# The out-projection of two attention layers in seven block products instead of eight

## What is computed

```python
h = rms_norm(x, norm_g[i]); proj = h @ w_in[i]
...
r_out = silu(rz) * retention(rotary(rq), rotary(rk), rv)
m_out = silu(mz) * moba(rms_norm(mq), rms_norm(mk), mv, rel_bias)
y = concatenate([r_out, m_out], axis=-1) @ w_out[i]
x = x + y
gate = sigmoid(rms_norm(x) @ w_ple_gate[i])
e = rms_norm(p[i] @ w_ple[i], ple_norm_g[i])
x = x + gate * e
```

## Time and profile before

| | |
|---|---|
| median of 3 runs | 1584.13 us (1581.85 to 1585.59) |
| the profiled execution, its own time | 1584.45 us |
| its span, first to last instruction | 1582.7 us |
| granted TensorE clock, mean | 0.952 of full speed |
| PE busy | 1331.9 us, 84% of the span |
| PEld (weight loads beside PE) | 717.9 us, 45% |
| DVE busy | 422.3 us, 27% |
| ACT busy | 278.8 us, 18% |
| POOL busy | 180.1 us, 11% |
| HBM read | 495.11 MB, 314 GB/s over the span |

### The profile page before, as it was taken

The page is one execution under the profiler, slowest core; times in us unless marked ns, Lnnn a source line. Parts: engine busy times, 40 slices in busy tenths (PEclk is TensorE's granted clock), DMA queues, the critical chain, the costliest instruction groups (busy, mean ns, idle before and its releaser), DMA issues. The chain is left out here.

```text
span 1582.7 us, 22176 instructions
## 1 busy us (share of the span) xinstructions
PE 1331.9 (84%) x9378; PEld 717.9 (45%) x9378; DVE 422.3 (27%) x838; ACT 278.8 (18%) x544; POOL 180.1 (11%) x122
## 2 busy tenths in 40 slices
PE   9999999999999999776776777899999676667676
PEld 4855456545869564322322323655654232232232
DVE  3443343523555531020000000257321000010011
ACT  2132310323413121210000000105211011011010
POOL 0450033300000005692000000000000000000000
PEclk9999999999999999899888899999999989899889
DMA  9923442244631489999999999944799999999997
GB/s 382 342 81 145 178 156 106 80 186 161 238 123 59 165 338 426 427 429 428 428 429 428 428 429 428 392 180 167 284 379 426 426 428 426 428 428 427 427 428 325
DMA packets 44868, 498.20 MB, mean 315 GB/s; under 512 B 6657, under 2 KB 8961, under 8 KB 12545
## 3 DMA queue, kind: packets, MB, share of 16 engines
q1 hardware_dynamic: 44800, 497.22, 76.7%
HBM read 495.11 MB, written 2.10 MB: 314 GB/s over the span
## 5 line engine op out<-in xcount | busy, mean ns | idle before, releaser
L2834 PE MATMUL banks<-weight_ring,arena 128*32 128x512 f32 x1472 | 214.6, 716 | 127.6 <-DMA weight_ring<-in_moe_weights 127.4
L2762 DVE TENSOR_TENSOR arena<-arena,banks 64x512 f32<-64x512 f32 x32 | 22.1, 690 | 665.3 <-ACT arena L2707 665.3
L2834 PEld LDWEIGHTS banks<-weight_ring,arena 128*32 128x32 f32 x1472 | 45.6, 120 | 283.9 <-DMA weight_ring<-in_moe_weights 142.2
L2819 PE MATMUL banks<-arena,x 128*128 128x64 f32 x1024 | 120.4, 277 | 0.0
L2819 PEld LDWEIGHTS banks<-arena,x 128*128 128x128 f32 x1024 | 119.7, 196 | 0.1
L323 PE MATMUL banks<-weight_ring,hT 128*128 128x512 f32 x256 | 114.0, 601 | 0.0
L2707 ACT ACTIVATE arena<-banks 64x512 f32<-64x512 f32 x32 | 18.9, 591 | 501.8 <-PE banks L2834 501.8
L2845 PE MATMUL banks<-weight_ring,arena 128*32 128x512 f32 x728 | 86.0, 596 | 22.2 <-DMA weight_ring<-in_moe_weights 10.2
L2875 PE MATMUL banks<-arena 64*128 64x512 f32 x240 | 59.6, 615 | 21.0 <-ACT arena L2713 21.0
L323 PEld LDWEIGHTS banks<-weight_ring,hT 128*128 128x128 f32 x256 | 48.7, 192 | 58.4 <-issue 58.0
L2834 PE MATMUL banks<-arena 128*32 128x512 f32 x352 | 58.6, 686 | 16.8 <-DMA arena<-in_moe_weights 16.8
(11 more groups left out here) (526 smaller groups left out, 1738.5 us busy)
## 6 DMA issues: line engine op xcount, KB each, us to landing
weight_ring<-in_moe_weights SPq DMA_DIRECT2D x137, 2048.0 KB, 27.0
weight_ring<-in_ring_weights SPq DMA_DIRECT2D x35, 2048.0 KB, 9.3
arena<-in_moe_weights SPq DMA_DIRECT2D x18, 2048.0 KB, 44.5
spare_weights<-in_moe_weights SPq DMA_DIRECT2D x10, 2048.0 KB, 43.9
mix<-in_moe_weights SPq DMA_DIRECT2D x9, 2048.0 KB, 48.2
arena<-in_moe_weights SPq DMA_DIRECT2D x17, 1024.0 KB, 42.2
x_normed<-in_moe_weights SPq DMA_DIRECT2D x9, 1024.0 KB, 39.1
hT<-in_moe_weights SPq DMA_DIRECT2D x9, 1024.0 KB, 47.5
```

Of the source, the lines that this page charges most:

```text
L2762: dve.tensor_tensor(hid[0:2 * CAP, :], sil[0:2 * CAP, :], b_gu[2 * CAP:4 * CAP, :], ALU.mult).then_inc(s_h, 1)
L2819: ins = pe.matmul((b_x, b_dn)[k // 4][:, k % 4 * 2 * CAP:(k % 4 + 1) * 2 * CAP], g.x[:, tt, k * P:(k + 1) * P], Pr[:, tt, :], start=(tt == ...
L2834: ins = pe.matmul(b_gu[q:q + CAP, :], xg[:, 2 * quarter + k, e * CAP:(e + 1) * CAP], up_w(where, quarter, e)[:, which, k, :], start=(quart ...
```

## The change

The out-projection is now itself one set of seven block products, `out_product` O1 to O7 of four matmuls each, with GpSimd forming four sums of the two weight chunks 8 and 9 (the same 128x2048 shape, into the ring and into T2 and T3), and four sums of mixT (SO1 to SO4, 128x512, in `rqk_flat`). O1 and O2 share bank 0, O6 and O7 use bank 1, O5 and O4 bank 4, O3 bank 5. ScalarE copies O1's block out (`y_p1_copy`); VectorE forms u_a and u_b and adds them and the products into x: nine additions of 128x512 in place of four. The two embedding products e_in(0) and e_in(1) move in between O2 and O6, and between O7 and the transposes. Gate products go to banks 0, 5, 4, 1. The right half of tile 1 is finished before its left half, and its squares are taken in that order. Places 8 and 9 of the ring are freed by O4 and O3.

```diff
--- before.py
+++ after.py
@@ -351,9 +351,9 @@
     def sems(g, name):
         return [g.sem(f"{name}_{k}") for k in ("squares", "eps", "root", "xs", "transposed", "hT")]
 
-    def squares(self, act, tt, ch):
+    def squares(self, act, tt, ch, place=None):
         half = slice(ch * HALF, (ch + 1) * HALF)
-        j = 2 * tt + ch
+        j = 2 * tt + (ch if place is None else place)
         act.activation(self.g.xs[:, tt, half], self.g.x[:, tt, half], ACT.Square,
                        accum_out=self.part[:, j:j + 1]).then_inc(self.s_sq.sem, 1)
 
...
@@ -407,12 +407,13 @@
...
-                 ("cd", "combined", 12), ("sl", "combined_used", 6), ("ts", "weight_sums", 8), ("as_", "input_sums", 4), ("rot", "rotated", 4), ("mean", "qk_mean", 2),
+                 ("cd", "combined", 12), ("sl", "combined_used", 6), ("ts", "weight_sums", 12), ("as_", "input_sums", 8),
+                 ("yc", "y_p1_copied", 1), ("u", "y_sums", 5), ("rot", "rotated", 4), ("mean", "qk_mean", 2),
...
-                 ("mix", "mixed", 2), ("mt", "mix_transposed", 4), ("mT", "mixT", 4), ("y", "y", 4), ("x", "x", 4),
+                 ("mix", "mixed", 2), ("mt", "mix_transposed", 4), ("mT", "mixT", 4), ("y", "y", 7), ("x", "x", 4),
...
@@ -497,7 +498,7 @@
     for l in range(DEPTH):
         q = layer[l]
         for i, when in enumerate((q.prj(3), q.prj(4), q.prj(6), q.prj(8), q.prj(15), q.prj(15), q.prj(22), q.prj(22),
-                                  q.y(3), q.y(4), q.e(4), q.g(3), q.g(4))):
+                                  q.y(7), q.y(5), q.e(4), q.g(3), q.g(4))):
             g.free_when[per * l + i] = when
 
 
@@ -517,7 +518,12 @@
                               (q.c11(1), formed(q, 0, C12), formed(q, 0, C21), formed(q, 0, C22)))
     gates_ready = lambda q: ((q.c11(2), q.sl(4), q.sl(6), q.sl(5)) if q is layer[0] else
                              (q.c11(2), q.sl(1), q.sl(3), q.sl(2)))
-    OUT_BANK = (0, 1, 4, 5)
+    GATE_BANK = (0, 5, 4, 1)
+    O1, O2, O6, O5, O3, O7, O4 = range(1, 8)
+    MX11, MX12, MX21, MX22 = (g.mixT[:, 4 * k:4 * k + 4, t * P:(t + 1) * P] for t in range(2) for k in range(2))
+    SO1, SO2, SO3, SO4 = (rqk_flat[:, i * 512:(i + 1) * 512].rearrange("p (k t) -> p k t", k=HT) for i in range(4))
+    u_a, u_b = tmp[:, 0:512], tmp[:, 512:1024]
+    X11, X12, X21, X22 = (g.x[:, tt, ch * HALF:(ch + 1) * HALF] for tt in range(2) for ch in range(2))
     part = lambda j: (slice(None), j // 2, slice((j % 2) * HALF, (j % 2 + 1) * HALF))
 
     with nc.Block() as block:
@@ -621,11 +627,15 @@
                 act.activation(eroot[:, tt:tt + 1], epart[:, 2 * tt + 1:2 * tt + 2], ACT.Sqrt,
                                bias=eeps[:, tt:tt + 1], scale=1.0 / D).then_inc(q.er.sem, 1)
 
+            def y_p1_copy(q):
+                act.wait_ge(*q.y(O1))
+                act.copy(u_a, ps[0]).then_inc(q.yc.sem, 1)
+
             def sigmoid(q, j):
                 act.wait_ge(*q.g(j + 1))
                 if j >= 2:
                     act.wait_ge(*q.gu(j - 1))
-                act.activation(sig[j % 2], ps[OUT_BANK[j]], ACT.Sigmoid).then_inc(q.gs.sem, 1)
+                act.activation(sig[j % 2], ps[GATE_BANK[j]], ACT.Sigmoid).then_inc(q.gs.sem, 1)
 
             for tt in range(TT):
                 act.wait_ge(s_x[tt], 16)
@@ -675,14 +685,20 @@
                 mix_copies(q, 0)
                 other_out(q, 1, C22)
                 other_out(q, 1, C21)
+                y_p1_copy(q)
                 mix_copies(q, 1)
-                for tt in range(TT):
-                    for ch in range(2):
-                        act.wait_ge(*q.x(2 * tt + ch + 1))
-                        n.squares(act, tt, ch)
-                    n.root(act, tt)
+                act.wait_ge(*q.x(1))
+                n.squares(act, 0, 0)
                 e_out(q, 0)
+                act.wait_ge(*q.x(2))
+                n.squares(act, 0, 1)
+                n.root(act, 0)
+                act.wait_ge(*q.x(3))
+                n.squares(act, 1, 1, 0)
                 e_out(q, 1)
+                act.wait_ge(*q.x(4))
+                n.squares(act, 1, 0, 1)
+                n.root(act, 1)
                 e_root(q, 0)
                 sigmoid(q, 0)
                 act.wait_ge(*q.gu(1))
@@ -744,9 +760,17 @@
                     dve.wait_ge(*formed(q, pair, {U4: U2, C12: U4, U3: U4, C22: C12, C21: U3}[n]))
                 TT_(out, in0, bank, ALU.subtract if n == C21 else ALU.add).then_inc(q.cd.sem, 1)
 
-            def add_out(q, j):
-                dve.wait_ge(*q.y(j + 1))
-                TT_(g.x[part(j)], g.x[part(j)], ps[OUT_BANK[j]], ALU.add).then_inc(q.x.sem, 1)
+            def out_sums(q):
+                dve.wait_ge(*q.y(O6))
+                dve.wait_ge(*q.yc(1))
+                TT_(u_a, u_a, ps[1], ALU.add).then_inc(q.u.sem, 1)
+                dve.wait_ge(*q.y(O5))
+                dve.wait_ge(*q.u(1))
+                TT_(u_b, u_a, ps[4], ALU.add).then_inc(q.u.sem, 1)
+                TT_(X21, X21, u_a, ALU.add).then_inc(q.u.sem, 1)
+                dve.wait_ge(*q.u(2))
+                TT_(X12, X12, u_b, ALU.add).then_inc(q.u.sem, 1)
+                TT_(X22, X22, u_b, ALU.add).then_inc(q.u.sem, 1)
 
             def e_eps(q, tt):
                 dve.wait_ge(*q.ec(4 * tt + 2))
@@ -849,14 +873,22 @@
                             ins.then_inc(q.mix.sem, 1)
                     dve.wait_ge(*q.mix(tt + 1))
 
-                add_out(q, 0)
+                dve.wait_ge(*q.y(O2))
+                TT_(X11, X11, ps[0], ALU.add).then_inc(q.x.sem, 1)
+                out_sums(q)
                 n.eps(dve, 0)
-                add_out(q, 1)
+                dve.wait_ge(*q.y(O3))
+                dve.wait_ge(*q.u(4))
+                TT_(X12, X12, ps[5], ALU.add).then_inc(q.x.sem, 1)
                 n.scale(dve, 0)
-                add_out(q, 2)
+                dve.wait_ge(*q.y(O7))
+                dve.wait_ge(*q.u(5))
+                TT_(X22, X22, ps[1], ALU.add).then_inc(q.x.sem, 1)
+                link(dve, TT_(X21, X21, ps[1], ALU.add))
                 n.evacuate(dve, 0)
                 n.eps(dve, 1)
-                add_out(q, 3)
+                dve.wait_ge(*q.y(O4))
+                TT_(X21, X21, ps[4], ALU.subtract).then_inc(q.x.sem, 1)
                 n.scale(dve, 1)
                 e_eps(q, 0)
                 e_normed(q, l, 0)
...
@@ -900,6 +932,23 @@
                         pool.tensor_tensor(S3, A11, A21, ALU.subtract).then_inc(q.as_.sem, 1)
                     pool.wait_ge(*done(q, pair, P2))
                     pool.tensor_tensor(wx[:, 4:8], T2, wx[:, 4:8], ALU.subtract).then_inc(q.ts.sem, 1)
+                wx, wy = (g.chunk(pool, per * l + c) for c in (8, 9))
+                pool.tensor_tensor(wy[:, 0:4], wy[:, 0:4], wx[:, 0:4], ALU.subtract).then_inc(q.ts.sem, 1)
+                pool.wait_ge(*q.ts(9))
+                pool.wait_ge(*done(q, 1, P6))
+                pool.tensor_tensor(T2, wy[:, 4:8], wy[:, 0:4], ALU.subtract).then_inc(q.ts.sem, 1)
+                pool.wait_ge(*q.ts(10))
+                pool.wait_ge(*done(q, 1, P7))
+                pool.tensor_tensor(T3, T2, wx[:, 0:4], ALU.subtract).then_inc(q.ts.sem, 1)
+                pool.wait_ge(*q.mT(4))
+                pool.tensor_tensor(SO1, MX21, MX22, ALU.add).then_inc(q.as_.sem, 1)
+                pool.wait_ge(*q.as_(5))
+                pool.tensor_tensor(SO2, SO1, MX11, ALU.subtract).then_inc(q.as_.sem, 1)
+                pool.wait_ge(*q.as_(6))
+                pool.tensor_tensor(SO4, MX12, SO2, ALU.subtract).then_inc(q.as_.sem, 1)
+                pool.tensor_tensor(SO3, MX11, MX21, ALU.subtract).then_inc(q.as_.sem, 1)
+                pool.wait_ge(*q.y(O2))
+                pool.tensor_tensor(wx[:, 4:8], T2, wx[:, 4:8], ALU.subtract).then_inc(q.ts.sem, 1)
 
         @block.tensor
         def _(pe):
@@ -941,6 +990,27 @@
                     ins = pe.matmul(at_ps[n - 1], left[:, k, :], right[:, k, :], start=(n != P2 and k == 0), stop=(k == HT - 1),
                                     skip_group_check=n in (P1, P2))
                 ins.then_inc(q.prj.sem, 1)
+
+            def out_product(l, n):
+                q = layer[l]
+                wx, wy = (g.chunk(pe, per * l + c) for c in (8, 9))
+                left, right, bank = {O1: (MX11, wx[:, 0:4], 0), O2: (MX12, wx[:, 4:8], 0), O6: (SO2, T2, 1),
+                                     O5: (SO1, wy[:, 0:4], 4), O3: (SO4, wy[:, 4:8], 5), O7: (SO3, T3, 1),
+                                     O4: (MX22, wx[:, 4:8], 4)}[n]
+                if n in (O5, O6, O7, O4):
+                    pe.wait_ge(*q.ts(8 + {O5: 1, O6: 2, O7: 3, O4: 4}[n]))
+                if n in (O5, O6, O3, O7):
+                    pe.wait_ge(*q.as_(4 + {O5: 1, O6: 2, O3: 3, O7: 4}[n]))
+                if n == O2:
+                    pe.wait_ge(*q.yc(1))
+                if n in (O5, O3):
+                    pe.wait_ge(*formed(q, 1, {O5: C21, O3: C22}[n]))
+                if n in (O7, O4):
```

(29 more changed lines are left out.)

6 lines of the change are left out of this document (3 added, 3 removed).

## The result

The changed kernel takes 1605.87 us (median of 4 runs, 1604.16 to 1607.67), the kernel before 1583.3 us beside it (1581.85 to 1585.59): a ratio of 1.0135, 95% interval 1.0119 to 1.0151. It is slower by 22.6 us, as forecast in sign, and beyond the forecast range's end of 1602.

A forecast was written before the change was run, and what follows sets the result against it. It took TensorE to bound the first layers and the DMA engines to bound the kernel later. Per layer -3.4 + 7.7 + 2.0 = +6.3 us, +12.6 for two, on 1584.45 gave 1597.0 us; range 1586 to 1602.

The forecast's parts named there:

- What it takes off TensorE: Out-projection: seven products of four matmuls in place of four of eight, saving 3.43 us per layer.
- The covers (a) to (e): First layers: GpSimd's mix sums, ScalarE's copy, VectorE's additions, bank changes and the later-freed ring chunk are hidden, cost 0.
- (f): Four GpSimd sums of weights, 4.5 us each: three right behind its last old sum, the last, for O4, at cost 0.
- The wait that (f) makes: Before the first mixed transposes: GpSimd's sums and VectorE's two-SBUF-input operations take turns, so TensorE stands 7.7 us per layer.
- Rival 1: First layers: no collision that matters, waits hidden in VectorE's slack, only the saving counts: 1577.6 us, chance 0.14.
- rivals 2 and 3: Other turns in VectorE's chain: VectorE keeps its turn, 1587.6 us, chance 0.10; worse turns, 1602 us, chance 0.08.
- The clock: Behind TensorE's wait in each layer the granted clock falls to half, costing 2.0 us per layer.
- The sum for the first layers: Saving, wait and clock together: +6.3 us per layer, +12.6 us for both layers.
- the first part: What bounds the kernel: first layers TensorE-bound, later DMA-bound; a first-layer shift moves the end one to one, nothing subtracted.

The follow-up runs named there:

- e3: Changed kernel with the three early GpSimd sums of weights cut to 8 columns, so its out-projection is not the reference's: 1585.55 us, ratio 1.0008.
- e6: e5 with 8 more small matmuls at the end of the first layers: 1574.49 us, ratio 0.9938.
- e7: Kernel before with 8 more small matmuls at the end of the first layers (30 for 22): 1579.94 us, ratio 0.9977.
- e2: Kernel before, eight products kept, with three GpSimd sums of the same size added where the change has them: 1604.53 us, ratio 1.013.
- e1: Changed kernel, three early weight sums moved: before pair 1's last sum, behind the first mixed tile, behind the sums of inputs: 1588.62 us, ratio 1.0024.
- e5: As e1, but with the first weight sum in front of pair 0's last sum instead of pair 1's: 1585.61 us, ratio 1.0009.
- e9: e6 with the second and third weight sums back right behind pair 1's last sum, the first still early: 1575.93 us, ratio 0.9946.
- e4: Changed kernel with 8 more small matmuls at the end of the first layers (30 for 22): 1593.66 us, ratio 1.0063.
- e10: Changed kernel with 4 more small matmuls at the end of the first layers (26 for 22): 1594.68 us, ratio 1.0065.
- e8: Kernel before with 8 fewer small matmuls at the end of the first layers (14 for 22): 1590.38 us, ratio 1.0046.

## Why the prediction was right and wrong

**What it takes off TensorE (3.43 us a layer): nearly right.** In the changed kernel itself, from O1 to the start of the next layer's products, 3.3 us (202.20 - 140.20 for 196.56 - 131.26). In e3, from P7 to the end of layer 0, 3.3 us; between e6 and e7, from layer 0's mixed transposes to the end of the layer, 3.0 (73.51 for 76.48 us), 0.3 of the difference being the late transposes above.

**The covers (a) to (e): right.** In the changed kernel O6 does not wait, SO2 being ready at 148.13 and O6 starting at 149.79; the copy of O1 costs O2 at most 0.06 us (144.60 for 143.67 + 0.87); X's additions hold nothing. Only when the sums are moved (e6) does (f)'s "VectorE has no operation on two SBUF tensors" stop being true.

**The wait that (f) makes (7.7 us): right in mechanism, place and size.** The chain went as worked out, turn by turn, to within half a microsecond: mix at 134.18 for 134.6; idle 7.32 us. e2 brings it into the kernel before, e1, e3, e5 and e6 take it away, e9 shows the slack of 2.1 us at work. The rule of the Trainium skill (SBUF — State Buffer, Who interferes with whom) holds in every place: operations with two SBUF inputs are held to the end of GpSimd's sum, and L761 with one input in PSUM took its 0.69 us under them. Rival 1 falls, and rivals 2 and 3, which had the turns go otherwise, are excluded by the rows of the changed kernel.

**The clock (2.0 us a layer): right.** The transposes and P4 took 0.89 + 0.77 us more in layer 0 (136.00 - 134.24 for 0.87, 140.20 - 136.00 for 3.43) and 0.89 + 0.95 in layer 1: 1.7 and 1.8 us. By the same rows it was 2.3 and 2.2 us in e4, with the same code there, and 2.2 and 2.0 in e2.

**The sum for the first layers, +12.6: measured +12.07.** Two parts of it are 5.8 us for layer 0 and 6.0 for layer 1 where I had 6.3 each; 0.4 is a longer wait in front of the even layer, which I had not in the sum. That the two agree to half a microsecond is in part luck: e4, which has the same code up to its 8 matmuls, comes to 13.3 us when these matmuls and the lag at 22 us are taken off.

**The step that failed** stands in the first part: "a shift of the first layers moves that stream and the end one to one; I subtract nothing for it." The stream of weights did move one to one or nearly (from +13.72 to +14.41 across the first experts). But the change also moves TensorE's instructions, and for that the prediction has no term at all: it put it at nothing without a reason. At two places in runs of very short matmuls TensorE then stops for 1.3 to 4.5 us, and the low clock behind costs nothing (e10) to 5.1 us (e3) more. This gave +5.2 us in the odd layer. That it goes with the place of the instructions is shown by e4, e6, e7, e8 and e10: 4 or 8 small matmuls more or less ahead move the time by 3.8 to 12.2 us; in e8 and e10 they move the even layer's pause by just as many passes, in e4, e6 and e7 it is gone; while a delay without a shift of code (e2) does not bring the odd layer's step. That what TensorE lacks there is the fetched block is read from the blocks' landings; no row shows where a block ends in the program or that TensorE waits for it. The remaining 2.3 us of the profiled execution are at the even layer's pause (+0.9, where the clock stayed low for longer) and in two more low stretches up to and in the first experts (+0.8 and +0.6); these go with the clock and differ from kernel to kernel (e2 has +1.5 at the pause). The median difference of 22.6 is 2.9 us more than that of the two profiled executions; where it lies in the other runs no trace says.

**What stays open:** why a block comes so late. In the changed kernel the weights' transfers kept the DMA engines busy up to 1055 us, and the block came with them; whether it was asked for late or held up by them, the runs don't tell. The place alone doesn't set the length: e2 and e10 both stop after 141 passes, for 3.61 and 1.48 us. It was not tried to keep transfers away from it.

## What to carry to other kernels

Before handing work to an idle GpSimd, list what VectorE does in those microseconds with two SBUF inputs (and its tensor_scalar operations, however small): each is held for the rest of a sum, they take turns, and the cost is the chain's total delay less its slack. As the Trainium skill puts it (SBUF — State Buffer, Summary: rules for kernel authors), schedule whichever is off the critical path; here the second and third held operation decided, and moving the sums by some microseconds turned +13.7 us into -5.4. And when a change adds or removes instructions ahead of runs of short matmuls, time it with a few dummy matmuls more or less before believing a difference under one per cent.

## What the runs showed that I had not expected

A pause of TensorE marked "issue", with no releaser, can go with an instruction fetch: the q8 block landed 1.3 us before TensorE went on, before and after the change. Eight matmuls of 0.22 us each (two passes of 0.11) at the end of the first layers took 3.8 us off the kernel before, 12.2 off the changed one and 11.1 off e5. And a tensor_scalar of two columns was held by GpSimd like a large operation, 2.60 us instead of 0.17.
